# Hybrid decoder trunk on one core: token routing in two tile groups, gate weights after the selection, token count read ahead of the expert loops, last expert step loaded in halves, filler matmuls ahead of the y transposes

## What is computed, cut to what matters

```python
logits = (xf @ router_w + router_b)
top_val, top_idx = lax.top_k(logits, 4)
gates = softmax(top_val)
# for each expert e and the tokens that chose it:
hb = x[tok] @ w1[e] + b1[e]                  # 1024 -> 2048
g, u = min(hb[:, :1024], 7), clip(hb[:, 1024:], -7, 7)
yb = (g * sigmoid(1.702 * g) * (u + 1)) @ w2[e] + b2[e]   # 1024 -> 1024
y[tok] += yb * gate
```

## Time and profile before

| | us |
|---|---|
| median of 3 runs | 1213.25 (1212.83 to 1213.63) |
| the profiled execution, its own time | 1214.7 |
| its span in the profile | 1212.9 |
| PE busy in it | 1144.4 |
| DVE, ACT, POOL busy | 365.3, 166.0, 140.5 |
| DMA | 430.13 MB, mean 355 GB/s |

### The profile page before, as it was taken

One profiled execution on the slowest core, in us unless ns is written; L12 is line 12 of the kernel. 1 busy time (PEld: TensorE's weight loads), 2 busy tenths in 40 slices (PEclk: granted clock), 3 DMA queues, 4 the chain that ended last, 5 costly groups with the idle time before them and its releaser, 6 DMA issues.

```text
span 1212.9 us, 13031 instructions
## 1 busy us (share of the span) xinstructions
PE 1144.4 (94%) x5046; PEld 480.0 (40%) x5046; DVE 365.3 (30%) x710; ACT 166.0 (14%) x315; POOL 140.5 (12%) x236
## 2 busy tenths in 40 slices
PE   7999877989999999999999999999999999999884
PEld 5767563453334333333433343333333332333221
DVE  5999873430212122131212121212121121202122
ACT  3312232111102010100110010102010100010002
POOL 6857853000000000000000000000000000000000
PEclk9999877978999999999999999999999999999998
DMA  7510643656999999999999999999999999999993
GB/s 223 198 46 1 208 162 134 216 224 250 427 427 426 427 427 427 427 428 428 428 428 428 428 428 428 428 428 428 428 428 428 428 428 428 428 428 427 427 427 122
DMA packets 78901, 430.13 MB, mean 355 GB/s; under 512 B 10714, under 2 KB 21186, under 8 KB 29714
## 3 DMA queue, kind: packets, MB, share of 16 engines
q1 hardware_dynamic: 78436, 428.47, 85.5%
q0 software_dynamic: 384, 1.18, 0.4%
q10 hardware_dynamic: 46, 0.01, 0.0%
HBM read 425.98 MB, written 3.67 MB: 354 GB/s over the span
## 4 chain that ended last, share of the span: by engine, by line
PE 68%; DVE 13%; DMA 8%; SPq 7%; issue 2%; ACT 1%; DVEq 0%; ACTq 0%
PE psum L1877 30%; PE psum L1887 14%; PE psum L1842 9%; SPq L360 6%; DMA ring_a<-in_exp_w_dram 5%; PE psum L1852 4%; DMA ring_b<-in_exp_w_dram 3%; PE psum L1739 2%; PE psum L1861 1%; PE psum L1898 1%; DVE ring_a L1140 1%; PE psum L1508 1%; DVE gsm L957 1%; PE psum L1730 1%; DVE ring_a L1136 1%
## 5 line engine op out<-in xcount | busy, mean ns | idle before, releaser
L1877 PE MATMUL psum<-ring_a,xg 128*64 128x512 f32 x1536 | 345.6, 599 | 7.8 <-DMA ring_a<-in_exp_w_dram 7.8
L1877 PEld LDWEIGHTS psum<-ring_a,xg 128*64 128x64 f32 x1536 | 105.5, 137 | 230.1 <-issue 213.2
L1887 PE MATMUL psum<-ring_a,aT 128*64 128x512 f32 x768 | 173.1, 597 | 8.3 <-DMA ring_a<-in_exp_w_dram 5.5
L1389 DVE TENSOR_TENSOR x<-x,psum 128x512 f32<-128x512 f32 x64 | 44.0, 687 | 365.7 <-PE psum L1852 365.7
L1842 PE MATMUL psum<-S,xn 128*128 128x256 f32 (+1 forms) x384 | 114.8, 429 | 1.2 <-DVE S L1377 1.2
L1877 PE MATMUL psum<-ring_b,xg 128*64 128x512 f32 x512 | 114.8, 595 | 0.2 <-DMA ring_b<-in_exp_w_dram 0.2
L1420 DVE TENSOR_SCALAR acts<-psum 128x512 f32<-128x512 f32 x32 | 22.0, 687 | 298.6 <-PE psum L1877 298.6
L1887 PEld LDWEIGHTS psum<-ring_a,aT 128*64 128x64 f32 x768 | 52.6, 136 | 110.0 <-issue 96.8
L1842 PEld LDWEIGHTS psum<-S,xn 128*128 128x128 f32 (+1 forms) x384 | 64.9, 195 | 57.3 <-issue 51.6
L1877 PEld LDWEIGHTS psum<-ring_b,xg 128*64 128x64 f32 x512 | 35.3, 137 | 73.6 <-issue 70.2
L865 ACT ACTIVATE acts<-acts 128x512 f32<-128x512 f32 x32 | 20.0, 626 | 316.6 <-DVE acts L1420 316.6
(11 more groups left out here) (414 smaller groups left out, 872.1 us busy)
## 6 DMA issues: line engine op xcount, KB each, us to landing
ring_a<-in_exp_w_dram SPq DMA_DIRECT2D x144, 2048.0 KB, 25.4
ring_b<-in_exp_w_dram SPq DMA_DIRECT2D x48, 2048.0 KB, 26.8
ring_a<-in_w_in_dram SPq DMA_DIRECT2D x5, 2048.0 KB, 8.6
ring_a<-in_w_out_dram SPq DMA_DIRECT2D x2, 2048.0 KB, 8.2
ring_a<-in_state_ml_c_dram SPq DMA_DIRECT2D x4, 512.0 KB, 6.2
out_dram<-ring_a SPq DMA_DIRECT2D x4, 512.0 KB, 3.2
xn<-in_x_prompt_dram SPq DMA_DIRECT2D x2, 512.0 KB, 4.2
ring_a<-in_w_in_dram SPq DMA_DIRECT2D x1, 1024.0 KB, 4.9
```

The lines of the kernel that those rows point to most:

```text
L1389: TT(dst, dst, psum[0:n, banks[c], :], ALU.add).then_inc(sem("combine_added"), 1)
L1877: m = M(psum[64 * x:64 * x + 64, bk, :], xg[:, k, u, 64 * x:64 * x + 64], w[:, 2048 * x + 512 * bk:2048 * x + 512 * bk + 512], start=False ...
L1887: m = M(psum[64 * x:64 * x + 64, 4 + nn, :], aT[:, 2 * j + s, 64 * x:64 * x + 64], w[:, 2048 * x + 1024 * s + 512 * nn:2048 * x + 1024 * s ...
```

## The change

PE: 28 filler matmuls ahead of the y transposes; the logits of tiles 0 and 2 are said to be ready by themselves, those of tile 1 go to a bank of their own; the fillers get 128 rows of ones instead of 96 rows of biases and are 9 and 5 instead of 14 and 8. DVE: the clearing of buffers goes ahead of the norm, tiles 0 and 2 are routed to their mask ahead of tile 1, the scaling of tile 1's rows goes behind `mask_ready`, all gate weights behind the selection and the count. SP, ACT and DVE read the count ahead of their first sweep. SP's last double pair is written out, and its last step loaded as two DMAs of 1 MiB, with PE's order of products changed to fit.

```diff
+_place([... "h2T3", "cum", "lg1"], range(6))
 # SP
+                if end:
+                    sp.dma_start(place[:, :, 0:1024], src[:, :, 0:1024]).then_inc(slot_filled(il)[0], 16)
+                    sp.dma_start(place[:, :, 1024:2048], src[:, :, 1024:2048]).then_inc(sem("end_filled"), 16)
...
+            sp.wait_ge(*at("count_ready", 1))
+            most = sp.value_load(cnt[0:1, 0:1], min_val=0, max_val=T)
             for il in range(DEPTH, 2 * STEPS):
                 sp.wait_ge(sem("step_done"), il + 1 - DEPTH)
                 load_step(il // STEPS, il)
-            with sp.Fori(1, NPAIR // 2) as q:
+            with sp.Fori(1, NPAIR // 2 - 1) as q:
+                load_pairs(q, q * (2 * STEPS))
+            load_pairs(NPAIR // 2 - 1, (NPAIR // 2 - 1) * (2 * STEPS))
 # ACT
-            sweep(0)
             act.wait_ge(*at("count_ready", 1))
             most = act.value_load(cnt[0:1, 0:1], min_val=0, max_val=T)
+            sweep(0)
 # DVE
+            dve.wait_ge(sem("logits_first"), 1)
+            for i in (0, 2):
+                ins_ = logits(i, bank("lg")[0:TILES[i][1], NE * i:NE * i + NE])
+                drains(ins_, "lg") if i == 2 else dv(ins_)
+            for i in (0, 2):
+                best(i)
+            dv(choose(slice(0, 3, 2), 2))
+            dve.wait_ge(*at("root2_ready", 3))
+            dv(V.reciprocal(st2[:, 5:6], st2[:, 5:6]))
+            await_fill(dve, "lg1")
+            drains(logits(1, bank("lg1")[:, 0:NE]), "lg1")
+            best(1)
+            says(choose(slice(1, 2), 1), "mask_ready", 1)
             says(TT(gk[:, :, 0:TOPK], top[:, :, 0:TOPK], spread(top[:, :, 0:1], 2, TOPK), ALU.subtract), "top_diff", 1)
+            for hf in range(2):
+                await_fill(dve, f"h2T{2 + hf}")
+            dv(TSC(xn[:, 1, :], xn[:, 1, :], st2[:, 5:6], None, ALU.mult))
...
             select(0).then_inc(sem("s_ready"), 1)
+            select_bias(0).then_inc(sem("selb_ready"), 1)
             dv(V.tensor_reduce(st2[:, 8:9], bank("cum")[:, 96:128], AX.X, ALU.max))
             says(V.tensor_copy(cnt[:], st2[:, 8:9]), "count_ready", 1)
+            dve.wait_ge(*at("top_exp", 1))
+            ... the gate weights, L1352 to L1361 of before ...
             dve.wait_ge(sem("s_ready"), 1)
+            most = dve.value_load(cnt[0:1, 0:1], min_val=0, max_val=T)
             sweep(0)
-            most = dve.value_load(cnt[0:1, 0:1], min_val=0, max_val=T)
 # PE
+            def keep_warm(n, bk):
+                for _ in range(n):
+                    M(psum[:, bk, :], ones_bf[:], spread(ones_bf[:].unsqueeze(1), 1, 4), start=True, stop=True)
+            await_bank(pe, "cu00")
+            keep_warm(28, FILLS["cu00"][0])
             for h in range(H):
                 pe.wait_ge(*at("y3_ready", h + 1))
...
-                    logits(i, hf)
+                    m = logits(i, hf)
+            m.then_inc(sem("logits_first"), 1)
+            pe.wait_ge(sem("logits_first"), 1)
+            pe.sem_inc(filled[FILLS["lg"][0]], 1)
             turn_rows(1, (1,))
+            await_bank(pe, "lg1")
             logits(1, 0)
-            ends_fill(logits(1, 1), "lg")
+            ends_fill(logits(1, 1), "lg1")
-            stay_busy(14)
+            stay_busy(9)
...
-                    for s, nn in ((0, 0), (0, 1), (1, 0), (1, 1)) if j < 3 else ((0, 0), (1, 0), (0, 1), (1, 1)):
+                    for s, nn in ((0, 0), (0, 1), (1, 0), (1, 1)) if j < 3 or ending else ((0, 0), (1, 0), (0, 1), (1, 1)):
+                        if ending and (s, nn) == (1, 0):
+                            pe.wait_ge(sem("end_filled"), t * 2 + (16 - 2 * (NPAIR // 2 - 1)))
...
-            stay_busy(8)
+            stay_busy(5)
             sweep(0)
```

More of the change, by code:

```diff
@@ L81 @@
 _place(["wo00", "wo01"], (4, 5))
-_place(["nT", "wo2", "wo10", "h2T0", "h2T1", "h2T4", "h2T5", "wo11", "h2T2", "lg", "h2T3", "cum"], range(6))
+_place(["nT", "wo2", "wo10", "h2T0", "h2T1", "h2T4", "h2T5", "wo11", "h2T2", "lg", "h2T3", "cum", "lg1"], range(6))
 SAID = {
@@ L350, in _, with load_step @@
         def _(sp):
-            def load_step(pair, il):
+            def load_step(pair, il, end=False):
                 which = il % STEPS
                 s, place = step_slot(il)
+                place = place.rearrange("p (x n) -> p x n", x=2)
                 if which < W1_STEPS:
@@ L472, in _ @@
                     with sp.If(most > r * SLOTS):
[L473 to L476, removed]
+                        with sp.Fori(0, NPAIR // 2 - 1) as q:
+                            load_pairs(q, r * (NPAIR * STEPS) + q * (2 * STEPS))
+                        load_pairs(NPAIR // 2 - 1, r * (NPAIR * STEPS) + (NPAIR // 2 - 1) * (2 * STEPS))
             for i in range(2):
@@ L1293, in _ @@
             dve.wait_ge(sem("stored"), 16 * 10)
+            dv(V.memset(lg[:], 0.0))
+            dv(V.memset(slot[:], 0.0))
+            dv(V.memset(sgate[:], 0.0))
             def weighted_half(i, c):
@@ L1329, in _ @@
                         weighted_half(i, c)
[L1331 to L1339, removed]
@@ L1340, in _, with logits @@
-            for i in range(3):
+            chosen = SG[:].rearrange("p i x s -> p i (x s)").rearrange("p i (k e) -> p i k e", k=TOPK)
+            weighted = yb[:].rearrange("p x n -> p (x n)")[:, 0:3 * TOPK * NE].rearrange("p (i k e) -> p i k e", i=3, k=TOPK)
+            by_choice = lambda v, i: spread(v[:, i, 0:TOPK].unsqueeze(3), 3, NE)
+            experts = lambda n: spread(spread(iota_e[:].unsqueeze(1).unsqueeze(1), 1, n), 2, TOPK)
+            def logits(i, view):
+                n = TILES[i][1]
+                return STT(out=lg[0:n, i, :], in0=view, scalar=st2[0:n, 4 + i:5 + i], in1=rbias[0:n, :], op0=ALU.mult, op1=ALU.add)
@@ L1341, in _, with best @@
+            def best(i):
                 dv(V.max(top[:, i, :], lg[:, i, :]))
                 dv(V.max_index(topi[:, i, :], top[:, i, :], lg[:, i, :]))
[L1343 to L1347 removed]
@@ L1348, in _ @@
[L1348 to L1354, removed]
@@ L1795, in logits @@
                 b, f = FILLS[f"h2T{2 * i + hf}"]
+                out = bank("lg1")[:, 0:NE] if i == 1 else bank("lg")[0:n, NE * i:NE * i + NE]
                 pe.wait_ge(drained[b], f + 1)
                 for k in range(4 * hf, 4 * hf + 4):
-                    m = M(bank("lg")[0:n, NE * i:NE * i + NE], h2T[:, k, t0:t0 + n], rw[:, k, :], start=(k == 0), stop=(k == KD - 1))
+                    m = M(out, h2T[:, k, t0:t0 + n], rw[:, k, :], start=(k == 0), stop=(k == KD - 1))
                 return m
@@ L1861, in bias, with pair_steps @@
                 return M(psum[:, bk, :], selb[0:96].rearrange("p x s -> p (x s)"), bsplit[0:96, col:col + 512], start=True, stop=False)
-            def pair_steps(gp, t, u, first=False, onward=False):
+            def pair_steps(gp, t, u, first=False, onward=False, last=False):
                 def await_step(w):
@@ L1955, in two_pairs @@
                 pair_steps(t * 2, t, 0, first=first)
-                pair_steps(t * 2 + 1, t, 1, onward=not last)
+                pair_steps(t * 2 + 1, t, 1, onward=not last, last=last)
             def sweep(t0):
```

34 lines of the change are left out of this document (21 added, 13 removed).

## The result

Four runs of the changed kernel have a median of 1201.49 us (1199.31 to 1202.17), four of the kernel before on the same chip 1213.04 us (1212.3 to 1213.63). The ratio is 0.9899 (95% interval 0.9887 to 0.991): 11.6 us faster, 1.0%. The forecast was 1197, so the direction and the place were right, and the time came out 4.5 us above it. The profiled execution of the kernel after took 1201.55 us (span 1199.7) where that of before took 1214.7 (span 1212.9): 13.15 us.

What follows compares the result with a forecast made beforehand. The weight stream at 427 to 428 GB/s bounds the kernel, so only time before 281 us and behind 1191 us counts; 1.9 + 3.4 + 9.0 + 1.2 + 0.9 = 16.4 us off 1213.25 gives 1197 us, range 1193.5 to 1206.5.

Steps and rivals of the forecast that it cites:

- The frame: Weight stream: from the first freed load (281.27) to the last step's start (1190.93) stays 909.7 us, before and after.
- C: Expert gather, bias and first three steps: PE keeps full clock, 9.0 us won; 1 in 4 that it is lost, then 0.
- B: Routing between logits and gather: the gather can start at 257.6 instead of 260.98, 3.4 us won.
- D: Kernel's end: last step loaded in halves wins 1.2 us, the count's read moved off DVE's last chain wins 0.9.
- The price of halves: Last step's two 1 MiB DMAs: extra cost between 0 and 1.2 us, taken as 0 because they stand in a full queue.
- A: 28 fillers ahead of the y transposes: less half clock behind them, bounds 0 and 3.9 us, middle 1.9 taken.
- the prediction's own sign: Output products behind the y transposes: if the six still take 5 us, the y fillers' forecast gain is wrong.
- That execution was 1.45 us above the median of the runs: Sum: the profiled execution's 1214.7 less 16.4 gives 1198.3; against the runs' median of 1213.25, 1197 us.
- Rival 1: Clock lost again before the gather, so nothing won there: 1205.9 us, chance 0.25.
- Rival 2: Loads of steps 2 and 3, issued after w_out_used, come late and swallow the gain before 281 us: 1211.2, chance 0.05.
- Rival 3: SP's written-out last double pair gets instructions late and starves the load queue: slower, 1275 with three stops a step; chance 0.03.
- a rule: y transposes: a transpose doesn't count as PE-busy the same way; strictly, the clock falls inside them, y fillers worth about 1.

## Why the prediction was right, and where it was short

**The frame held.** First freed load to last step was to stay at 909.7 us; the stretch to the last step but one is 904.81 before and 904.85 to 905.18 in the three profiles cited above.

**C, the clock in the gather: forecast 9.0, measured 8.9** (20.29 to 11.40; against the second profile of before, 19.46, it is 8.1). The chance of 1 in 4 that it is lost again didn't come up in any of the nine profiles that keep the new order with its fillers; of the 43 runs of these kernels one, at 1209.6, looks as if it had lost it. Of the reasons given, that there must be fillers is shown. That the stretch is fuller or the holes shorter is shown only in part: with the old stretch the denser rows held the clock in five of seven runs, with the new one the thinner rows did in four of four, and what in the new order does it (its length, its holes or the time at which it stands) no run separates.

**B, routing: forecast 3.4, measured 3.14.** The holes ahead of the counts and of the gather are 0.73 and 0.51 us. DVE started on the logits 1.1 us later than the step said (250.01 to 251.10 on its own clock; the whole timeline had shifted by that 1.05 at tile 1's projection, 239.62 to 240.67), and the counts came 1.2 later (256.43 for 255.2), so within the section the working was good to 0.3.

**D, the end: forecast 1.2 and 0.9, measured 1.42 and 1.12** in the two profiles (1.43 and 0.94 by the single edits; 0.84 for the read against the mean of the profiles). The chain of waits of after shows it:

```profile
1143.42 31.92 DMA ring_b<-in_exp_w_dram
1175.47 7.09 PE psum L1933 x32
1182.56 3.65 PE psum L1895 x8
1188.69 2.79 issue
```

The price of halves, for which I kept 0 against a bound of 1.2, is nothing that the rows show. The Trainium skill (DMA: Bandwidth & Descriptors, Bandwidth) gives 341 GB/s for 1 MB by itself; the estimate from it that left 0.6 of the 1.2 doesn't hold for two halves that stand in a full queue, and the trace decides. PE meets the second half without a hole.

**A, the fillers: forecast 1.9, and around it lies what was missed.** Its own size is inside the bounds of 0 and 3.9: 1.72 in the two first profiles, some 0.8 on the mean of all; that the first pair comes so near to 1.9 is luck of where the falls lay. The term was too large because its lower bound, "the fillers may only move the fall some us later", was nearer than the middle: the fall is there in all eight profiles with just the 28, and begins 12.4 to 13.7 us behind the start of the gate products instead of 6.0 to 7.1. By the prediction's own sign, six output products that still take 5 us, A was wrong in four of the eight.

Two costs stood in no term. Between the transpose of n and DVE's first addition 1.62 us were added. What stands there is a DVE that waits for DMAs, and behind it the three clearings, which the sum had moved for nothing: at 233.65 DVE is the late engine, and nothing covers them. They cost 0.65, the later landing about 1.0. This is no part of A that failed to reach the routing: without the y fillers the section is as long (8.2 us). And the later rows made a hole of 1.45 us among PE's transposes. In five of the seven profiles with the clearings in front the clock fell between 239.7 and 242.1, which cost 1.65 to 1.7 us (19.9 instead of 18.2 to the gather). In the three with the clearings back it didn't. That the hole is the cause fits, but two of the seven had it and kept the clock, so it makes the fall likely, not certain.

**The sum.** Forecast 16.4 against 13.15 in the profiles: 1.47 short in A, 0.26 in B, 0.11 in C, 0.37 in the stream, 0.44 over in D the other way, and 1.48 that came from ahead of the change. The rest of the 4.5 us is the step "That execution was 1.45 us above the median of the runs": I took the first profile's offset for a property of the kernel and of both versions. The profile of after sits on its median (1201.55, 1201.49). By the means of all profiles, an estimate: A 1.1 short, 1.6 for the late DVE and 1.2 for a fall that costs 1.7 in five of seven, together 3.9 of the 4.5. Both profiled executions of the kernel before came out at 1214.7; why, I can't say.

**The rivals.** Rival 1 (cold gather) is real, and is what the run without routing fillers and two of the seven runs of the old order with new rows show. Rival 2 (loads of steps 2 and 3 late) didn't occur: the first freed load moved 10.98 us forward, and the 48 instructions of the first three steps stand in one row of 10.52 us. Rival 3 (SP's straight code starves the queue) didn't occur: the stream is within 0.37 us of what it was.

For the transposes I had weighed a rule: what the clock does while PE transposes. With ten more fillers the transposes run 1.12 and 1.13 us at full clock and nothing falls. With the 28 alone the clock fell inside the second group of transposes in four of the eight profiles, and 0.1 to 0.7 us behind its end in the other four. The rule of the Trainium skill (TensorE: Matmul & The Clock Gate, Part 4), taken strictly, would have let the clock fall inside them; with fillers right before and between them it doesn't, and no run here tells what transposes without fillers around them would do.

## What to carry to other kernels

When steps are moved, look at the engine that is late by itself at their new place: here PE won up to 1.7 us, and DVE, which waited for DMAs and had three small clearings put in front of it, lost 1.6 beside it. What stands between a wait and the first instruction whose result another engine needs is not free, be it 0.2 us long. When fillers are to hold a clock, look at the whole stretch up to the next dense work and fill the small holes behind them too; and judge by several runs, since a clock that is held mostly shows as two levels of time (here about 1204 and 1213 us).

## What the runs showed that I had not expected

- Ten fillers in two holes of 1.4 and 1.2 us, on top of the 28, gave more than the 28 in the hole of 7.4 us had given: 1.7 us (17.90 to 16.21 from the gate products to the first update, against the run with only the shorter waits) against some 0.8.
- The clock fell in other places from run to run of one program: profiled executions of nearly the same kernel lost it at 196 to 199 us (190 to 194 without the 28 fillers) and at 240 to 242 us, with the fillers each time for 3 to 7 us, or not at all there. Single runs of one program lie up to 4 us apart without any change of the code.
- PE was busy for 18.0 of the 19 us from 260 to 279 at 0.50 in the kernel before. In its two profiles and in the one without routing fillers the clock stayed at 0.50 for 20.5 us, through the whole gather and into the first steps. Where it fell 1.65 us into the gather (the old order with new rows) it stayed there for 13.6 us.
- Between DVE's last copy and the end of its branch 2.7 to 3.05 us pass even when the count is already in a register; the read is only 0.8 to 0.9 of the former 3.7 to 3.9.
- Two small DMAs landed about 1 us later after their issue in the changed order (4.03 instead of 2.98 us for the last store of `xn` in the first two profiles, 5.1 to 6.0 instead of 4.2 to 4.3 for the router's bias in all). The cause is open.
